# A two-block transformer kernel: second merge and query product in rounded parts, tokens loaded first, last results turned early

## What is computed

```
hn = rms_norm(x, ln_gain)                     # first block
z  = hn @ w_in + b_in
...
mod = silu(c) @ w_mod + b_mod                 # second block, 96 chunks of 128
merged = sigmoid(ga) * (ya @ w_branch_a) + sigmoid(gb) * (yb @ w_branch_b)
x  = x + g1 * (merged @ w_out)                # "second merge", then "out2"
h  = rmsnorm(x, norm2_w) * (1 + sc2) + sh2
q  = h @ w_q                                  # "peer_q", the query product
...                                           # scores, top 16, 128 x 128 experts
x  = x + g2 * experts
out = rmsnorm(x, final_norm_w)
```

## Time and profile before

| | us |
|---|---|
| median of 3 runs | 4605.21 (4604.98 to 4606.14) |
| profiled execution, its own time | 4608.16 |
| its span, first to last instruction | 4606.4 |
| PE busy with products | 4275.7 (93%) |
| DVE busy | 2876.4 (62%) |
| ACT busy | 1897.9 (41%) |
| mean granted PE clock | 0.969 of full speed |

### The profile page before, as it was taken

One profiled execution on the slowest core, in us unless ns is written; L12 is line 12 of the kernel. 1 busy time (PEld: TensorE's weight loads), 2 busy tenths in 40 slices (PEclk: granted clock), 3 DMA queues, 4 the chain that ended last, 5 costly groups with the idle time before them and its releaser, 6 DMA issues.

```text
span 4606.4 us, 64970 instructions
## 1 busy us (share of the span) xinstructions
PE 4275.7 (93%) x26784; PEld 3780.7 (82%) x26784; DVE 2876.4 (62%) x4644; ACT 1897.9 (41%) x3029; POOL 0.2 (0%) x4
## 2 busy tenths in 40 slices
PE   5999879999999989789998998998899999999997
PEld 5999868998988876678877987887688888888886
DVE  6888754666777653557765200487667666676665
ACT  3444464433452333444433001146455545555453
POOL 0000000000000000000000000000000000000000
PEclk9999989999999999989998998999999999999998
DMA  6888433367754432200003453424365554545542
GB/s 253 315 310 309 173 117 131 127 223 263 274 199 185 165 129 75 83 1 1 1 1 141 147 184 110 160 110 192 137 242 195 194 219 174 228 191 198 217 173 90
DMA packets 135906, 764.23 MB, mean 166 GB/s; under 512 B 12240, under 2 KB 29776, under 8 KB 66128
## 3 DMA queue, kind: packets, MB, share of 16 engines
q1 hardware_dynamic: 135632, 760.32, 44.3%
HBM read 737.20 MB, written 23.07 MB: 165 GB/s over the span
## 4 chain that ended last, share of the span: by engine, by line
PE 80%; DVE 10%; ACT 4%; DMA 3%; issue 1%; SPq 0%; DVEq 0%; ACTq 0%
PE ps L3222 14%; PE ps L3198 9%; PE ps L320 5%; PE ps L822 5%; PE ps L3200 5%; PE ps L824 5%; PE ps L823 5%; PE ps L875 4%; PE ps L877 4%; PE ps L876 4%; PE ps L2868 2%; PE ps L2677 1%; PE ps L3126 1%; PE ps L2680 1%; PE ps L3118 1%
## 5 line engine op out<-in xcount | busy, mean ns | idle before, releaser
L3222 PE MATMUL ps<-pieces,gact_parts 128*128 128x512 f32 x3072 | 713.3, 393 | 27.3 <-DVE pieces L3294 15.9
L3222 PEld LDWEIGHTS ps<-pieces,gact_parts 128*128 128x128 f32 x3072 | 578.5, 189 | 154.8 <-issue 20.3
L3198 PE MATMUL ps<-hp_parts,pieces 128*128 128x512 f32 x1792 | 635.5, 399 | 15.3 <-DVE pieces L3294 15.3
L824 PE MATMUL ps<-x_rounded,ring_rounded 128*128 128x256 f32 x2000 | 564.2, 282 | 0.0
L3200 PE MATMUL ps<-hp_parts,pieces 128*128 128x256 f32 x1792 | 503.7, 281 | 0.0
L3294 DVE TENSOR_TENSOR pieces<-ring,pieces 128x512 fp32r<-128x512 f32 x448 | 309.7, 692 | 268.7 <-ACT pieces L3239 268.7
L3294 DVE TENSOR_TENSOR pieces<-area,pieces 128x512 fp32r<-128x512 f32 x512 | 351.7, 689 | 181.6 <-ACT pieces L3239 173.2
L3239 ACT ACTIVATE pieces<-area 128x512 fp32r<-128x512 f32 x512 | 320.8, 629 | 339.2 <-PE ps L3222 204.6
L3239 ACT ACTIVATE pieces<-ring 128x512 fp32r<-128x512 f32 x448 | 282.9, 632 | 342.9 <-PE ps L3200 264.3
L3198 PEld LDWEIGHTS ps<-hp_parts,pieces 128*128 128x128 f32 x1792 | 337.4, 188 | 99.3 <-issue 15.5
L824 PEld LDWEIGHTS ps<-x_rounded,ring_rounded 128*128 128x128 f32 x2000 | 381.0, 190 | 0.0
(11 more groups left out here) (495 smaller groups left out, 8657.0 us busy)
## 6 DMA issues: line engine op xcount, KB each, us to landing
ring<-u_dram SPq DMA_DIRECT2D x128, 1024.0 KB, 6.5
area<-v_dram SPq DMA_DIRECT2D x128, 1024.0 KB, 8.7
ring<-w_mod_dram SPq DMA_DIRECT2D x96, 1024.0 KB, 7.0
ring<-w_mg_dram SPq DMA_DIRECT2D x80, 1024.0 KB, 4.8
ring<-w_z_dram SPq DMA_DIRECT2D x77, 1024.0 KB, 6.8
ring<-w_branch_dram SPq DMA_DIRECT2D x80, 512.0 KB, 3.6
ring<-w_out_dram SPq DMA_DIRECT2D x32, 1024.0 KB, 4.9
ring<-w_y_dram SPq DMA_DIRECT2D x20, 1024.0 KB, 4.8
```

The lines of the kernel that those rows point to most:

```text
L824: return nc.tensor.matmul(out, rest, hn_rounded[:, k, :], start=False, stop=last)
L3198: both = nc.tensor.matmul(bank(s).rearrange("p (a t) -> p a t", t=T), piece[:, b, 0, k * P:(k + 1) * P], hp2[:, :, c, :], start=(c == 0), ...
L3222: last = nc.tensor.matmul(out, gact[:, k, ga, s, t * P:(t + 1) * P], piece[:, b, va, :], start=(s == 0 and w == 0), stop=(s == GROUP - 1 a ...
```

## The change

The new weights path of the second merge, out2 and peer_q is the split one. The activations are split too: the two branch results in quarters during the first gate blocks of `merge2_act` and `merge2_dve`, the merged chunks while the merge runs, the normalised chunks one by one. The norm's sums for x are made between out2's blocks. At the start the tokens are loaded first in quarters, squared in quarters, and scaled, rounded and split in quarters; cond_tanh and cond_silu come behind. At the end half of the transposes stand ahead of the last group's last column, half of the residual steps ahead of the last add, squares follow chunk by chunk, and the result is stored in four parts. Several stages share semaphores with earlier ones. The core of the diff, changed lines with the heads of their functions:

```diff
         def pre_act(act):
-            act.wait_ge(inputs_loaded, N_INPUTS * 16)
...
         def n1_act(act):
+            norm = Do(act, st_n1, "act")
+            for q in range(4):
+                act.wait_ge(x_landed[q], 16)
+                v = slice(4 * q, 4 * q + 4)
+                norm("squares" + (str(q) if q < 3 else ""), nc.scalar.activation(sq[:, v, :], xc[:, v, :], ACT.Square))
+            round_z(act, 0)
+            norm.wait("pe", "sums")
+            act.wait_ge(norm_inputs, 32)
+            norm("root", nc.scalar.activation(root, bank(4, 0, T), ACT.Sqrt, bias=par("eps"), scale=1.0 / D))
+            norm.end()
...
-            round_z(act, 0)
...
+            pre_act(act)
+            act.wait_ge(inputs_loaded, N_INPUTS * 16)
...
         def n1_pe(pe):
-            norm_pe(pe, st_n1, 0, sq, bank(4, 0, T), DC)
-            barrier(pe, "norm_x", "hn_split")
+            do = Do(pe, st_n1, "pe")
+            pe.wait_ge(norm_inputs, 32)
+            for q in range(4):
+                do.wait("act", "squares" + (str(q) if q < 3 else ""))
+                for c in range(4 * q, 4 * q + 4):
+                    last = nc.tensor.matmul(bank(4, 0, T), ones, sq[:, c, :], start=(c == 0), stop=(c == DC - 1))
+            do("sums", last)
+            do.end()
...
+                elif b == 1:
+                    pe.wait_ge(inputs_loaded, N_INPUTS * 16)
...
+                    if b == 0 and k % 4 == 0:
+                        S["hn_split"].upto(pe, "dve", f"l{k // 4}", 0)
...
         def n1_dve(dve):
+            dve.wait_ge(norm_inputs, 32)
+            norm, do = Do(dve, st_n1, "dve"), Do(dve, st_hn, "dve")
...
+            norm.wait("act", "root")
+            norm("inverse", nc.vector.reciprocal(root, root))
+            norm.own()
+            for q in range(5):
+                for c in range(4 * q, min(4 * q + 4, DC)):
+                    norm(f"scaled{c}", nc.vector.scalar_tensor_tensor(out=hn[:, c, :], in0=xc[:, c, :], scalar=par("ln_gain", c), in1=root, op0=ALU.mult, op1=ALU.mult))
+                if q:
+                    v = slice(4 * q - 4, 4 * q)
+                    do.wait("act", f"r{q - 1}")
+                    do(f"l{q - 1}", nc.vector.tensor_tensor(hn_rest[:, v, :], hn[:, v, :], hn_rounded[:, v, :].bitcast(F32), ALU.subtract))
+            norm.end()
...
+            pre_dve(dve)
...
+        def round_last(act, b):
+            act.wait_ge(weights_used, last_at(b - 2) + 1)
+            round_block(act, last_at(b), LAST_PIECES + 2 * b, gate_rounded)
+        def split_last(dve, b):
+            split_block(dve, last_at(b), LAST_PIECES + 2 * b, gate_rounded)
+        def round_branch2(act, b):
+            at = streams["branch2"].first + b
+            act.wait_ge(landed[at % SLOTS], (at // SLOTS + 1) * 16)
+            nc.scalar.activation(ring_rounded[:, at % SLOTS, 1024:2048], raw_piece(at, 0), ACT.Copy).then_inc(weights_rounded, 1)
+        def split_branch2(dve, b):
+            at = streams["branch2"].first + b
+            dve.wait_ge(weights_rounded, BRANCH2_PIECES + b + 1)
+            nc.vector.tensor_tensor(rest_piece(at, 0), raw_piece(at, 0), ring_rounded[:, at % SLOTS, 1024:2048].bitcast(F32), ALU.subtract).then_inc(weights_split, 1)
...
+            for u in range(2 * DC):
+                at, j = streams["branch2"].first + u, u % 2
+                if u < 2:
+                    S["branch2_split"].upto(pe, "dve", f"l{2 * j + 1}", 0)
...
+                    S["merge2"].upto(pe, "dve", f"g{j}", (u - 4) // 2)
+                pe.wait_ge(weights_split, BRANCH2_PIECES + u + 1)
+                out = bank(u % 4, 0, T)
...
+                    w, w_rest = (v[:, k * P:(k + 1) * P] for v in (ring_rounded[:, at % SLOTS, 1024:2048], rest_piece(at, 0)))
+                    nc.tensor.matmul(out, w, branch2_in[:, j, k, :], start=(k == 0), stop=False)
+                    nc.tensor.matmul(out, w, branch2_rest[j][:, k, :], start=False, stop=False)
+                    last = nc.tensor.matmul(out, w_rest, branch2_in[:, j, k, :], start=False, stop=(k == BC - 1))
...
-            streams["branch2"].each(pe, part, step=32)
-            barrier(pe, "merge2")
-            gemm(pe, "out2", DC, lambda k: merged2[:, k, :])
+            pe.wait_ge(gates_kept, N_GATES + N_GATES2)
+            norm = Do(pe, st_np, "pe")
+            for b in range(DC):
+                if b >= SLOTS:
+                    pe.wait_ge(evacuated, evacuated_from["out2"] + b - SLOTS + 1)
+                for k in range(DC):
+                    if b == 0:
+                        S["merged2_split"].upto(pe, "dve", f"l{k}", 0)
+                    last = split_products(pe, bank(4 + b % SLOTS, 0, T), last_at(b), LAST_PIECES + 2 * b, gate_rounded, k,
+                                          hcat_rest[:, 0, k, :], merged2_rest[:, k, :])
+                last.then_inc(weights_used, 1)
+                if b >= 2:
+                    token_sums(pe, norm, b - 2)
...
         def merge2_act(act):
+            barrier(act, "dn_gate")
+            do = Do(act, st_branch2, "act")
...
+                q = i - GATES2_REST
+                if q < 4:
+                    do(f"r{q}", nc.scalar.activation(branch2_in[:, q // 2, 4 * (q % 2):4 * (q % 2) + 4, :], branch2_source(q), ACT.Copy))
...
+            do.end()
+            do = Do(act, st_merged2, "act")
+            def merged2_rounded(c):
+                S["merge2"].upto(act, "dve", "a1", c)
+                do(f"r{c}", nc.scalar.activation(hcat_rest[:, 0, c, :], merged2[:, c, :], ACT.Copy))
+            for b in range(2 * DC):
+                round_branch2(act, b)
+                if b % 2 == 0 and b >= 4:
+                    merged2_rounded((b - 4) // 2)
+            round_last(act, 0)
+            merged2_rounded(DC - 2)
+            merged2_rounded(DC - 1)
+            round_last(act, 1)
+            do.end()
+            norm = Do(act, st_np, "act")
+            for b in range(DC):
+                if b + 2 < DC + 1:
+                    round_last(act, b + 2)
+                act.wait_ge(evacuated, evacuated_from["out2"] + b + 1)
+                norm(f"square{b}", nc.scalar.activation(psq[:, b, :], xc[:, b, :], ACT.Square))
...
+            round_last(act, DC + 1)
...
         def merge2_dve(dve):
+            do = Do(dve, st_branch2, "dve")
...
+                q = i - GATES2_REST - 1
+                if 0 <= q < 4:
+                    do.wait("act", f"r{q}")
+                    v = slice(4 * (q % 2), 4 * (q % 2) + 4)
+                    do(f"l{q}", nc.vector.tensor_tensor(branch2_rest[q // 2][:, v, :], branch2_source(q), branch2_in[:, q // 2, v, :].bitcast(F32), ALU.subtract))
+            do.end()
...
+            for b in range(2):
+                split_branch2(dve, b)
...
+            rest = Do(dve, st_merged2, "dve")
+            def merged2_remainder(c):
+                rest.wait("act", f"r{c}")
+                rest(f"l{c}", nc.vector.tensor_tensor(merged2_rest[:, c, :], merged2[:, c, :], hcat_rest[:, 0, c, :].bitcast(F32), ALU.subtract))
...
+                    if idx + 2 < 2 * DC:
+                        split_branch2(dve, idx + 2)
...
+                if dc:
+                    merged2_remainder(dc - 1)
+            split_last(dve, 0)
+            merged2_remainder(DC - 1)
+            rest.end()
+            split_last(dve, 1)
...
-            add_block(dve, "out2", lambda i: xc[:, i, :], scalar=lambda i: modv[:, i + 2 * DC, 0:1])
+            for b in range(DC):
+                dve.wait_ge(weights_used, last_at(b) + 1)
+                nc.vector.scalar_tensor_tensor(out=xc[:, b, :], in0=bank(4 + b % SLOTS, 0, T), scalar=modv[:, b + 2 * DC, 0:1], in1=xc[:, b, :],
+                                               op0=ALU.mult, op1=ALU.add).then_inc(evacuated, 1)
+                if b + 2 < DC + 1:
+                    split_last(dve, b + 2)
...
         def choose_act(act):
-            barrier(act, "out2")
-            norm_act(act, st_np, 0, xc, psq, proot, bank(4, 0, T), T, 1.0 / D)
-            barrier(act, "norm_p")
...
+                S["norm_p"].upto(act, "dve", f"scaled{c}", 0)
...
-            do.end()
-            copy_out(act, "peer_q", lambda i: pq[:, i, :], T)
+                do.own()
+                do(f"hi{c}", nc.scalar.activation(hp_hi[:, c, :], hp[:, c, :], ACT.Copy))
+            do.end()
+            for b in range(DC):
+                act.wait_ge(weights_used, streams["peer_q"].first + b + 1)
+                nc.scalar.activation(pq[:, b, :], bank(b % SLOTS, 0, T), ACT.Copy).then_inc(evacuated, 1)
+                if b + 2 < DC:
+                    round_last(act, DC + b + 2)
...
         def choose_pe(pe):
-            barrier(pe, "out2")
-            norm_pe(pe, st_np, 0, psq, bank(4, 0, T), DC)
-            barrier(pe, "norm_p", "shift2")
-            gemm(pe, "peer_q", DC, lambda k: hp[:, k, :])
+            S["norm_p"].upto(pe, "act", "root", 0)
+            for b in range(DC):
+                if b >= SLOTS:
```

(66 more changed lines are left out.)

113 lines of the change are left out of this document (60 added, 53 removed).

## The result

The changed kernel takes 4522.24 us (median of 4 runs, 4520.90 to 4526.04) against 4605.68 for the kernel before on the same chip (4 runs, 4604.98 to 4609.19): a ratio of 0.9819, 95% interval 0.9802 to 0.9836. In the two profiled executions the span falls from 4606.4 to 4519.1 us, by 87.3.

What follows compares the result with a forecast made beforehand. The prediction took TensorE (PE), holding 80% of the last-ending chain, as the bound; gains of 13.5 + 12.3 + 14.9 + 33.3 + 13.9 = 87.9 us from 4605.2 gave 4517 us, range 4503 to 4532.

Steps and rivals of the forecast that it cites:

- start: Start and z stage: PE begins z at about 27 instead of 54.8, but DVE's order leaves 13.5 us gain.
- second merge and w_out: Both products in rounded parts, 90.4 us each instead of 110.5 and 110.8: gains of 12.3 and 14.9 us.
- hand-over and query product: From w_out's end through the query product: 109.2 us instead of 142.5, a gain of 33.3 us.
- end: After the last expert product: earlier transposes, sums without rest and a quarter's store last gain 13.9 us, bounds 11 and 17.
- full head start: Rival at the start: PE keeps its whole 27 us because DVE catches up; 4504 us, chance 10%.
- With four signals 2.9 us idle: Ahead of the w_out product: PE waits 2.9 us for g1, a1, one remainder and half of split_last(0).
- each restart of the clock: After the waits before the merge and before w_out: slow PE clock costs 1.5 us each, bounds 0 and 2.9.
- The rule weighed in the prediction: Skill's formula, 109 ns per 256-column product against the trace's 0.1178 us; would finish the 2304 new products 20 us sooner.
- denser: Rival for the new rounded products: 0.1067 us each, half the slow spacing, 26 us less; 4491 us, chance 3%.
- Fed late: Rival in the second merge: PE waits for DVE's remainders as in the first merge; 4526 to 4530 us, chance 12%.
- Slow clock: Rival in the new rounded stages: short waits halve PE's clock, 0.2133 us a product; up to 4737 us, chance 3%.

Runs made afterwards that it cites:

- mods_late: Changed kernel with the first mod chunk's loads and sums moved from z block 0 to 3, tanh and silu behind z block 3's remainders: 4517.64 us.
- x_late: Changed kernel with the 2 MB residual load moved behind the loads of w_out blocks 0 and 1: 4517.02 us, ratio 0.9796 to the kernel before.
- query_plain: Changed kernel with the query product on unrounded weights and queries, one product instead of three: 4538.27 us, ratio 0.9850 to the kernel before.

## Why the prediction was right

It said 4517 us, 4503 to 4532, and faster than before; 4522.24 came, in the range, with a ratio whose interval (0.9802 to 0.9836) is clear of 1. The steps, by the profiled executions:

| step | forecast | measured | by |
|---|---|---|---|
| start | 13.5 | 14.35 | z block 76 |
| second merge and w_out | 27.2 | 22.9 | 195.4 us forecast (99.4 + 90.4 + 5.6), 199.6 measured (2541.52 to 2741.07) |
| hand-over and query product | 33.3 | 33.4 | 109.2 us forecast, 109.1 measured |
| end | 13.9 | 15.0 | 37.9 - 21.1 - 1.8 |
| not forecast: first merge and before | 0 | 3.2 | 17.57 - 14.35 |
| not forecast: scores and expert stage | 0 | -1.6 | 73.94 at the last query copy, 72.3 at the last addition but one (4563.08 and 4490.74) |
| sum | 87.9 | 87.3 | spans: 87.3 |

The prediction's sums come out when redone, but for two last digits: w_out is 110.8 - 90.4 - 5.6 = 14.8 and not 14.9, and 2811.34 + 112.64 - 2781.3 is 142.7 and not 142.5 (142.5 is what the copies give, 2924.11 - 2781.57).

*Start.* The order on DVE held as worked out: first mod_chunk at 44.21 (forecast 44.1), split_z(1) at 34.05 to 36.4 (36.1), PE's wait ahead of block 2 8.2 us (some 8). The full head start (10%) did not come; mods_late shows that this order was what stood against it in blocks 2 to 4: with the chunks moved, z ends 22.0 us earlier than before.

*Second merge and w_out.* This is where the size was off. "With four signals 2.9 us idle" took w_out block 0 to have landed; it came behind the residual, and PE stood 5.1. And 1.5 us was taken for each restart of the clock: the merge's first units lost 2.5 (from the first product at 2544.35, 32 units at 2.83 would end at 2634.8, and the last ended at 2637.2), w_out's first block 2.4 (from 2642.3 to 2650.6 are 8.3, less 5.65 and 0.3 to the addition). 2.2 + 1.0 + 0.9 is 4.1 of the 4.2 that are missing. The size of the restart varies: with the same wait of 2.9 us ahead of it, the rounded merge took 87.2 to 89.2 us from first to last multiply by a gate in twelve executions. The price per product held: x_late's merge has 87.2 us for 31 x 24 products, 0.1172 each; w_out's blocks are (2741.07 - 2650.59)/15 = 6.03 apart, forecast 6.1. The rule weighed in the prediction (the Trainium skill, TensorE: Matmul & The Clock Gate, Back-to-back issue gap, 109 ns alone) stays below what any of these streams does; the rival "denser" found nothing in the traces.

*Hand-over and query product.* From the last addition (2741.07) to the last copy (2850.17) 109.1 us. Block 0 went at 0.92 us a chunk (forecast about 1.0), and the clock stayed at 0.50 from 2747 to 2766; the later blocks are 5.7 apart. So the slow clock reached over block 0 into the next, for which the sum had 2 us. query_plain confirms the price, and the rest of the 33.3 is the hand-over.

*End.* Gains as forecast, 1.1 more: a quarter's store lands 2.7 us after its issue, I took 3.6. By the Trainium skill (DMA: Bandwidth & Descriptors, Anatomy of one DMA), whose fit is for DMAs that GpSimd issues, while SP issues here, an estimate is 3.2: nearer, but still above the trace.

*Rivals.* "Fed late" needed waits of DVE all through the merge; there is one of 2.9 us at its start, and no other. "Slow clock" came only at the head of each stage, for 2.4 to 2.5 us in the merge and in w_out.

*What luck there was.* The sums agree within 0.6 us because the unforecast 3.2 us ahead of the gates and the missing 4.2 nearly cancel. Without the 3.2 the measured sum is 84.1, near the 83.4 of the medians, which is 4.5 below the forecast.

## What to carry to other kernels

When a product is turned into rounded parts, its own price is soon known; look then at the first operand of each stage: who loads, rounds and splits it, and what stands ahead of that on SP, ACT and DVE. Here two such places held 15 us more (7.7 at the end of z, and 7.0 between merge and w_out): the tanh, silu and chunks of other work ahead of the third and fourth block's remainders, and a 2 MB load and half a remainder ahead of the first weights. And an earlier start is worth only what the engine behind it can follow: of the 27 us at the start 14 were left at the end of z.
